# Attention of two heads side by side, values made once, gate and query tiles between the steps

## What is computed

```
q = rms_norm(q_a, g) @ w_q_b                   # 8 heads, 64 plain + 32 rotary columns
c_kv = rms_norm(kv_a[..., :256], g)
kv = c_kv @ w_kv_b                             # 8 heads, 64 key + 64 value columns
s = q_nope . k_nope + q_rope . k_rope          # rotary key shared by the heads
p = softmax(s * 96 ** -0.5)
att = (p @ v) @ w_mla_o                        # latents see latents + context, context sees context
x = x + g1 * ((g_att * att + g_conv * y_conv + g_sc * y_sc) @ w_o)
```

## Time and profile before

| | us |
|---|---|
| median of 3 runs | 1411.33 |
| profiled execution | 1412.78 |
| its span | 1410.9 |
| PE busy | 1297.5 (92%) |
| DVE busy | 652.1 (46%) |
| ACT busy | 540.9 (38%) |
| POOL busy | 391.8 (28%) |

### The profile page before, as it was taken

How to read it: one execution, slowest core, us unless ns; L and a number is a source line. 1 busy time by engine, 2 the same in 40 slices (tenths; PEclk the granted TensorE clock), 3 DMA queues, 4 the chain that set the end, 5 groups by cost and what they waited for, 6 DMA issues and landing times. The chain is left out here.

```text
span 1410.9 us, 21168 instructions
## 1 busy us (share of the span) xinstructions
PE 1297.5 (92%) x7310; PEld 1059.8 (75%) x7310; DVE 652.1 (46%) x1088; ACT 540.9 (38%) x883; POOL 391.8 (28%) x221
## 2 busy tenths in 40 slices
PE   4599999999999979999999999689999887899997
PEld 1377777767776857788778877569787887899996
DVE  1544676654234353222222233467766344744444
ACT  2343355443224233321232123336555443544443
POOL 3142111111222412222222223424112355344444
PEclk9699999999999989999999999889999998899998
DMA  8455311214555406742574256235222465466652
GB/s 291 142 179 177 88 46 52 60 38 120 149 157 164 149 1 193 210 149 72 168 207 150 75 166 196 73 75 134 80 75 74 128 184 150 118 197 179 179 167 72
DMA packets 271025, 186.39 MB, mean 132 GB/s; under 512 B 8379, under 2 KB 257521, under 8 KB 270961
## 3 DMA queue, kind: packets, MB, share of 16 engines
q1 hardware_dynamic: 270961, 185.52, 45.0%
HBM read 184.45 MB, written 1.05 MB: 131 GB/s over the span
## 5 line engine op out<-in xcount | busy, mean ns | idle before, releaser
L302 POOL TENSOR_TENSOR Wlo<-Wraw,Whi 128x1024 fp32r<-128x1024 f32 (+1 forms) x152 | 322.8, 2126 | 843.1 <-ACT Whi L291 842.3
L1318 PE MATMUL bank<-Hhi,Whi 128*128 128x256 f32 (+2 forms) x1200 | 412.0, 343 | 15.4 <-DVE Wlo L302 6.9
L1320 PE MATMUL bank<-Hhi,Wlo 128*128 128x256 f32 (+2 forms) x1200 | 405.8, 338 | 0.0
L1319 PE MATMUL bank<-Hlo,Whi 128*128 128x256 f32 (+2 forms) x1200 | 405.8, 338 | 0.0
L291 ACT ACTIVATE Whi<-Wraw 128x1024 fp32r<-128x1024 f32 (+3 forms) x336 | 278.5, 851 | 258.4 <-PE bank L1320 139.1
L302 DVE TENSOR_TENSOR Wlo<-Wraw,Whi 128x1024 fp32r<-128x1024 f32 (+4 forms) x184 | 182.2, 1008 | 305.3 <-ACT Whi L291 304.8
L1318 PEld LDWEIGHTS bank<-Hhi,Whi 128*128 128x128 f32 (+1 forms) x1200 | 227.8, 190 | 66.2 <-issue 30.9
L1320 PEld LDWEIGHTS bank<-Hhi,Wlo 128*128 128x128 f32 (+1 forms) x1200 | 227.8, 190 | 25.7 <-issue 0.8
L1319 PEld LDWEIGHTS bank<-Hlo,Whi 128*128 128x128 f32 (+1 forms) x1200 | 228.0, 190 | 24.4 <-issue 1.3
L1318 PE MATMUL bank<-Uhi,Whi 128*128 128x512 f32 (+1 forms) x544 | 187.3, 344 | 3.3 <-DVE Ulo L916 2.3
L1319 PE MATMUL bank<-Ulo,Whi 128*128 128x512 f32 (+1 forms) x544 | 183.8, 338 | 0.0
(11 more groups left out here) (129 smaller groups left out, 1391.3 us busy)
## 6 DMA issues: line engine op xcount, KB each, us to landing
Wraw<-in_w_ff SPq DMA_DIRECT2D x120, 512.0 KB, 4.8
Wraw<-in_w_in SPq DMA_DIRECT2D x78, 512.0 KB, 4.0
ATT<-in_w_mod SPq DMA_DIRECT2D x72, 512.0 KB, 4.7
ACC<-in_w_mod SPq DMA_DIRECT2D x20, 512.0 KB, 6.3
Wraw<-in_w_o SPq DMA_DIRECT2D x16, 512.0 KB, 4.4
Wraw<-in_w_ff SPq DMA_DIRECT2D x16, 384.0 KB, 4.0
Wraw<-in_w_mla_o SPq DMA_DIRECT2D x8, 512.0 KB, 3.4
Wraw<-in_w_q_b SPq DMA_DIRECT2D x8, 288.0 KB, 2.9
```

The source lines that it names most:

```text
L302: last = eng.tensor_tensor(lo, raw, hi.bitcast(F32), ALU.subtract)
L1318: pe.matmul(dst, sh, mh, start=j == 0, stop=False)
L1319: pe.matmul(dst, sh, ml, start=False, stop=False)
L1320: last = pe.matmul(dst, sl, mh, start=False, stop=j == k - 1)
```

## The change

- `V` becomes a tile of its own for all eight heads, over the memory of `SQ` and `TG`. A new chunk "values" (two DMAs per layer that pick every second 64 columns of `w_kv_b`) comes first, and four value tiles of 512 columns are made before the pairs. A layer then has 145 chunks. The key chunk of a pair is loaded as before, but only its 256 key columns are split.
- A step (duo) is now both heads of the pair at once, with 128 queries: four in layer 0, two in layer 1. Per step TensorE turns head 0, makes the next step's scores of head 0, the same for head 1, then one values' product in which the two heads alternate block by block, head 0 on columns 0 to 63 and head 1 on columns 64 to 127.
- The next pair's key tile and query tiles stand between the steps of this pair, as do the parts of the two gate tiles. The rotary part of the next pair's queries is computed at the end of this pair on VectorE.
- The score matmul takes 96 rows instead of 128.
- On ScalarE a step's copies alternate with the exponentials of the next; behind step 0 stand the tanh of the first gate and a `look`. On VectorE the taps spread over the steps, one before the first gate's `look` and the rest at the end.
- The pair loops of SyncE, ScalarE, VectorE and GpSimd are two turns (SyncE's still three) and the last two pairs stand behind; TensorE's is written out.
- `w_mla_o`: in the first of four chunks both tiles are made together, and the wait for the last attended block comes only before that block.

The core of the diff (`...` marks what is left out):

```diff
-PAIR_KINDS = ["keys", "queries", "plain", "plain"]
+HEAD_KINDS = ["values", "keys", "queries"]
+def pair_looks(p):
+    if p < PAIRS - 2:
+        return ["plain", "plain", "keys", "queries"]
+    return ["plain"] * (4 if p == PAIRS - 2 else 2)
...
+        V = sb("V", [P, 4, HEADS * VH])
+        SQ, TG = V[:, 0:2, :], V[:, 2:4, :]
...
+                values()
+                keys(0)
+                queries(0)
                 with at.loop(sp, PAIRS - 1, chunks=4) as i:
-                    pair(i)
-                pair(PAIRS - 1)
+                    gate(i, 0)
+                    keys(i + 1)
+                    queries(i + 1)
+                    gate(i, 1)
+                for j in range(2):
+                    gate(PAIRS - 1, j)
...
+                    for _ in exps(0):
+                        pass
+                    look(next(looks))
+                    gate_a = at.tile()
+                    for d in range(len(duos) - 1):
+                        for _ in zip(copies(d), exps(d + 1)):
+                            pass
+                        if d == 0:
+                            gate_out(gate_a, p * 2)
+                            look(next(looks))
+                    following = None
+                    if not last:
+                        following = [at.tile() for _ in range(3)]
+                        keys_out(following[0])
+                        for h in range(2):
+                            queries_out(h, following[1 + h])
+                    for _ in copies(len(duos) - 1):
+                        pass
+                    if not last:
+                        look(next(looks))
+                        look(next(looks))
...
+                    soften(0)
                     do_taps(1)
-                    for u in range(2, len(units)):
-                        row_max(u)
-                        normalise(u)
-                    do_taps(TAPS_PER_PAIR - 3)
...
+                    look(next(looks))
                     at.tile()
+                    for d in range(1, len(duos)):
+                        soften(d)
+                        if d < 3:
+                            do_taps(1)
+                        if d == 1:
+                            look(next(looks))
+                    if not last:
+                        at.tile()
+                        rope_queries()
+                        look(next(looks))
+                        do_taps(1)
+                        look(next(looks))
+                    for w in taps:
+                        tap(p * (2 * TAPS_PER_PAIR) + (CDW + 2 * w), p * TAPS_PER_PAIR + w)
...
+                def attend(p, d):
+
+                    col, k0, kt = duos[d]
+                    if d == 0 and p:
+                        pe.wait_ge(op_lo, at.operand.n)
+                    pe.wait_ge(turned_copied, at.unit.n + 2 * d + 2)
+                    for k in range(kt):
+                        for h in range(2):
+                            last = pe.matmul(PV[h * VH:(h + 1) * VH, col:col + P],
+                                             V[:, k0 + k, (2 * p + h) * VH:(2 * p + h + 1) * VH],
+                                             PTs[:, h, k * P:(k + 1) * P], start=k == 0, stop=k == kt - 1)
+                    last.then_inc(pv_done, 1)
+
+                for p in range(PAIRS):
+                    at.ring = 0
+                    scores(0, 0)
+                    scores(0, 1)
+                    more = p < PAIRS - 1
+                    if l == 0:
+                        gate_a = gate_parts(4, 8)
+                        gate_b = gate_parts(2, 4, 8) if more else gate_parts(1, 3, 5, 6, 8)
+                    else:
+                        gate_a = gate_parts(8)
+                        gate_b = gate_parts(2, 4, 8) if more else gate_parts(4, 6, 8)
+                    next(gate_a)
+                    for d in range(len(duos) - 1):
+                        for h in range(2):
+                            turn(d, h)
+                            scores(d + 1, h)
+                        attend(p, d)
+                        if d == 0 and l == 0:
+                            next(gate_a)
+                        elif not more:
+                            next(gate_b)
+                        else:
+                            if d == 1 or l == 1:
+                                keys = keys_tile()
+                                slot = chunk()
+                                query_tile(0, slot)
+                            if d == 2 or l == 1:
+                                query_tile(1, slot)
+                    d = len(duos) - 1
+                    turn(d, 0)
+                    next(gate_b)
+                    turn(d, 1)
+                    next(gate_b)
+                    attend(p, d)
+                    for _ in gate_b:
+                        pass
...
+                        if ready and j == 3:
+                            pe.wait_ge(op_lo, ready)
```

More of the change, by code:

```diff
@@ L107, in __init__ @@
     def __init__(self):
-        self.chunk, self.tiles, self.operand, self.unit, self.square, self.heads, self.gates, self.mod = (Tally() for _ in range(8))
-        self.turn = 0
+        self.chunk, self.tiles, self.operand, self.unit, self.duo, self.square, self.heads, self.gates, self.mod = (Tally() for _ in range(9))
+        self.turn = self.layers = 0
         self.uses = [Tally() for _ in range(4)]
@@ L508, in _ @@
                     step_in()
-                with at.loop(pool, PAIRS - 1, chunks=4):
-                    for kind in ahead(PAIR_KINDS, PAIR_KINDS):
+                for kind in ["plain", "keys", "queries"]:
+                    look(kind)
+                with at.loop(pool, PAIRS - 2, chunks=4):
+                    for kind in pair_looks(0):
                         look(kind)
-                for kind in ahead(PAIR_KINDS + ["plain"] * 4, branch_kinds(l)):
+                for p in range(PAIRS - 2, PAIRS):
+                    for kind in pair_looks(p):
+                        look(kind)
+                for kind in ahead(["plain"] * 4, branch_kinds(l)):
                     look(kind)
@@ L668, in _, with keys_out @@
                     mod_row()
[L669 to L676, removed]
+                duos = duos_of(l)
+                def keys_out(t):
                     act.wait_ge(tile_done, t.done)
@@ L725, in pair @@
                     act.activation(Uhi[:, p + AT0, 0:TQ], PV[:, 0:TQ], ACT.Copy).then_inc(op_hi, 1)
                     at.operand.next()
[L728 to L730 removed]
+                    gate_out(gate_b, p * 2 + 1)
+                    at.unit.n += 2 * len(duos)
+                    at.duo.n += len(duos)
+                with at.loop(act, PAIRS - 2, chunks=4, tiles=5, units=2 * len(duos), duos=len(duos), operands=1) as i:
+                    pair(i)
@@ L1145, in pair @@
                     at.tile()
                     low(Ulo[:, p + AT0, 0:TQ], PV[:, 0:TQ], Uhi[:, p + AT0, 0:TQ])
-                steps = 2 + 2 * TAPS_PER_PAIR + len(units)
-                with at.loop(dve, PAIRS - 1, chunks=4, tiles=6, units=len(units), operands=1, heads=2,
+                    at.unit.n += 2 * len(duos)
+                steps = 2 + 2 * TAPS_PER_PAIR + 2 * len(duos)
+                with at.loop(dve, PAIRS - 2, chunks=4, tiles=5, units=2 * len(duos), operands=1, heads=2,
                              extra=[(step, steps)]) as i:
-                    pair(i, PAIR_KINDS)
@@ L1550, in _, with keys_tile @@
-                pe.wait_ge(op_lo, at.operand.n)
-                with at.loop(pe, PAIRS - 1, chunks=4, tiles=6, units=len(units), operands=1, heads=2) as i:
-                    pair(i)
-                pair(None)
-                pe.wait_ge(op_lo, at.operand.n)
-                def mla():
-                    slot = chunk()
-                    for q in range(2):
-                        _, last = gemm(slot, 2 * CW, q * P, P, 4, O, AT0, TQ)
-                        last.then_inc(tile_done, 1)
+                def keys_tile():
+                    t, last = gemm(chunk(), P, 0, P, 2, O, CT0, T)
+                    last.then_inc(tile_done, 1)
+                    return t
```

357 lines of the change are left out of this document (172 added, 185 removed).

## The result

| | before | after |
|---|---|---|
| median, same chip, 8 runs each, us | 1412.24 | 1419.0 |
| ratio, 95% interval | | 1.0046 (1.0036 to 1.0055) |
| span of the profiled execution, us | 1410.9 | 1417.5 |
| mean granted clock | 0.967 | 0.957 |

What follows compares the result with a forecast made beforehand. PE, nearly unbroken, was taken to bound both layers' attention. Terms +2.2 - 7.9 + 1.6 - 9.0 + 2.5 = -10.6 us gave 1402.2 against the profiled 1412.78, so a 1401 us median; range 1388 to 1414.

Steps and rivals of the forecast that it cites:

- What is late next: Attention pairs: PE's own work plus waits for ScalarE and VectorE, 35.1 us a pair in layer 0, 20.2 in layer 1.
- The clock: Attention pairs: short, close waits cause one more clock dip in all, +2.5 us; bounds 0 and +18.
- Rival 4: Clock dips in most pairs and table loads behind the wait: 1415 to 1418 us, half staying near the old time; 10%.
- the table's loads: ScalarE's pair loop: its 1.28 us table reload goes ahead of the first exponential's wait, 0; if behind, +5 us.
- rival 3: Values' product in attention: the two heads' halves don't run beside one another, 1417 us; 12%.
- sign of being wrong as a whole: Attention: layer 0's pairs below 31 us or layer 1's above 23 would show the prediction wrong as a whole.
- The rotary chunk: Layer 1's projection: GpSimd splits this chunk, removing PE's 6.9 us wait and a half-clock tile, -9.0 us; bounds 0 to -9.5.
- PE's terms: PE's attention queue: values 5.5 us once a layer, halves fully overlapped, product 3.1 and 2.0 us a pair.
- the rule on row groups: Values' product: skill's rule that weight loads overlap a running matmul only in different row groups, so halves would gain nothing.
- Layer 1: Layer 1's attention: 10.4 + 3 x 20.2 + 19.0 = 90.0 us against 97.9, -7.9.
- The convolution's tail: After attention: VectorE enters this tail 0.4 and 1.2 us later relative to PE, which waits for it, +1.6 us.
- Rival 1: The steps hide everything: VectorE and ScalarE keep up and PE's queue counts in full, about 1370 us; 8%.

Runs made afterwards that it cites:

- the split cut short: The changed kernel, with GpSimd forming the low part of only 64 of a gate chunk's 1024 columns in both layers' attention: 1395.1 us, ratio 0.9886.
- the taps moved in layer 1: The changed kernel with TensorE's tile work ahead of the products and VectorE's taps behind steps 1, 2 and 3 in both layers: 1383.2 us, ratio 0.981.
- full width: Each values' product pass over all 128 columns, head after head: in the changed kernel 1431.1 us; with tile work ahead and taps moved in layer 0, 1382.9 us.
- the best kernel: The changed kernel with TensorE's tile work ahead of the products in both layers and VectorE's taps behind steps 1, 2, 3 in layer 0 alone: 1376.2 us, ratio 0.9754.

## Why the prediction was wrong, step by step

**The step that failed is "What is late next"**: there a tap stands at 1.4 us in layer 0, from the mean of the earlier trace rows, and with it a pair at "29.4 + 5.7 = 35.1". Pairs took 39.55, 38.92, 39.99 and 35.11. The tap behind step 0 stands just where GpSimd splits the pair's second gate chunk, since ScalarE makes that chunk's high part at the same place, and it took 3.50. I had the row for this, a 0.42 us sum that took 1.88 beside a GpSimd split, and used it to price a dip of the clock, not to ask which VectorE instructions of the new order would stand beside which split. The stage took 165.6 us against 149.4. With the split cut short it takes 149.6, but by errors that cancel: PE is idle for 21.8 us where the sum held 25.8 (three pairs with 5.7, the last with 8.1, 0.6 for the rotary wait), and 5.5 us go to the low clock, which the sum had elsewhere.

**The clock** (+2.5, one dip more) is the other term that failed, by its size: layer 0's attention alone lost 11.7 us to the low level, 1.00 granted before and 0.93 after, a little more than half of it with the collision. So the stage's miss of 16.2 is 5.8 more waiting (31.6 against 25.8), 11.7 of clock, and 1.3 less for the matmuls themselves. The upper bound of +18 held the truth, the chosen value did not. Rival 4 gave nearly the right time, 1415 to 1418, and half of the cause; it named no place for the trigger, and the table's loads did not stand behind the wait.

The signs on record misled: a layer-0 pair over 37 us was to decide for rival 3 ("the halves don't run beside one another"), and three pairs were over it though the halves do; and neither sign of being wrong as a whole came.

**Right:**
- The rotary chunk, in the main: -7.1 in the stage of the trace and -8.9 alone in before, forecast -9.0. From turn to total 9.1 us were gained; 0.6 of the 2 us given back is the next total, which waits 3.4 us for GpSimd's sums instead of 2.8.
- PE's terms: values 24 x 0.227 = 5.5 us; product 16 passes in 1.03; halves beside one another, so rival 3 fell. For the halves the Trainium skill ("TensorEngine Tiling (Array Packing)", Key Properties) says that different tiles load and multiply in parallel; the rows go with that, and not with the rule on row groups as the prediction read it.
- PE's largest waits in attention are those for ScalarE's copies, as named.
- Layer 1: 92.2, forecast 90.0, and 89.7 without the collisions. Ten taps of the last pair take 6.15 us there, beside a 2.45 us split.
- The table's loads, each at the head of an exponential, went ahead of the wait: 208.89, 1.28 us, done before the maximum. The convolution's tail: from the first matmul of `w_mla_o` to the first of the branches -0.5 us in layer 0 and +2.0 in layer 1, together +1.5, forecast +1.6.

Rival 1, "everything hidden", 1370, was given 8%. As a forecast for this order it was wrong, but it is within 0.5% of what the same work takes (1376) once the tile work stands in front of the waits. The forecast took the order as it was and counted 5.7 us of waits a pair in it, correctly but for the collision (the second pair of after has 8.0); it did not say that this was what the change left undone.

**Not settled:** what the taps moved in layer 1 cost. In the traces it is 3.1 us: the first transposes of its last three pairs wait 2.60, 2.70 and 4.46 us for VectorE instead of 1.30, 1.28 and 3.54. By the ratios (0.981 and 0.9754) it is 0.56%, 7.9 us, and the rest isn't explained. How the loss splits between waits and clock rests on PE's busy time in the windows, not on a run with the clock held.

## What to carry to other kernels

When work moves on VectorE, write down for each of its instructions with two SBUF inputs which GpSimd instruction stands beside it in the new order: the collision costs the tail of GpSimd's instruction, and what is queued behind pays (here maximum, exponential, copy, product, clock). Put TensorE's independent tile work in front of an instruction that waits for a chain through two other engines, not behind it: the same instructions, in another order, were 2.3% faster here (1.0046 to 0.982). And a longer pass does not cost its own time everywhere, since a wait behind it can take it back: full width, 14.2 us of passes, cost 14.4 us in after and 6.1 in the best kernel.

## What the runs showed of the hardware

- The second instruction of a tap (two SBUF inputs), started while a GpSimd split of 2.56 us ran, ended 0.55 us behind it, and the tap took 3.50 us instead of 1.41; a row maximum out of PSUM beside a split was not held (0.69 us).
- Two 128x64 halves in turn, 16 passes: 0.064 us a pass; the same passes head after head 0.095, full width 0.106 to 0.118.
- An idle time of 3.1 us in front of a product was followed by 0.52 granted. The best kernel, with no wait above 1.9 us in layer 0's attention, kept 1.00 through all of it. Short waits in front of the products alone don't do it: with the tile work ahead and the tap still in place those added up to 1.0 us, the transposes waited up to 4.1 us for VectorE, and the stage had 0.96.
